# Moving the token factor of a root-mean-square norm behind the matrix product it feeds, in an fp32 two-block transformer kernel

## What is computed

```python
def rms_norm(x, g):
    xf = x.astype(jnp.float32)
    xf = xf * lax.rsqrt(jnp.mean(xf * xf, axis=-1, keepdims=True) + EPS)
    return (xf * g.astype(jnp.float32)).astype(x.dtype)

x = x + rms_norm(mixed, norm1_post[i])
h2 = rms_norm(x, norm2_pre[i])
gate, up = jnp.split(h2 @ w_gate_up[i], 2, axis=-1)     # 1024 -> 2 x 2816
ffn = (jax.nn.silu(gate) * up) @ w_down[i]
x = x + rms_norm(ffn, norm2_post[i])
```

## Time and profile before

| What | Value |
|---|---|
| median of three executions | 2425.7 us (2420.35 to 2428.77) |
| profiled execution, its own time | 2425.2 us |
| span of its trace | 2423.4 us |
| TensorE busy | 2244.8 us, 93% of the span |
| VectorE, ScalarE, GpSimd busy | 46%, 41%, 40% |
| mean granted TensorE clock | 0.949 |
| share of the chain that ended last | TensorE 85%, VectorE 6%, ScalarE 4%, GpSimd 2% |

### The profile page before, as it was taken

One profiled execution on the slowest core, in us unless ns is written; L12 is line 12 of the kernel. 1 busy time (PEld: TensorE's weight loads), 2 busy tenths in 40 slices (PEclk: granted clock), 3 DMA queues, 4 the chain that ended last, 5 costly groups with the idle time before them and its releaser, 6 DMA issues.

```text
span 2423.4 us, 28048 instructions
## 1 busy us (share of the span) xinstructions
PE 2244.8 (93%) x10837; PEld 1837.0 (76%) x10848; DVE 1104.6 (46%) x1784; ACT 984.6 (41%) x1994; POOL 971.7 (40%) x754
## 2 busy tenths in 40 slices
PE   7999999999979887999999798996899997999997
PEld 6788778888867776788888675664687886888886
DVE  3544665553345764755443443445645224332322
ACT  5655444443245553344442354343344233332221
POOL 3654644333466642644334451003423335322232
PEclk9999999999989998999999898887999997999998
DMA  4111122222213220232322111000012221322221
GB/s 161 48 66 53 65 93 94 99 102 96 98 61 96 64 77 18 70 104 87 105 98 96 59 64 35 35 18 18 18 45 82 101 105 37 113 94 105 85 99 60
DMA packets 29845, 183.08 MB, mean 76 GB/s; under 512 B 3984, under 2 KB 4112, under 8 KB 11920
## 3 DMA queue, kind: packets, MB, share of 16 engines
q1 hardware_dynamic: 29712, 181.27, 21.6%
HBM read 174.97 MB, written 2.10 MB: 73 GB/s over the span
## 4 chain that ended last, share of the span: by engine, by line
PE 85%; DVE 6%; ACT 4%; issue 2%; POOL 2%; DMA 1%; SPq 0%; another core or an unknown queue 0%; POOLq 0%; ACTq 0%; DVEq 0%
PE PS L1284 83%; PE PS L1409 1%; PE PS L1519 1%; POOL LO L2486 1%; DVE bQS L1980 1%; POOL A_p L2506 0%; DMA RAW<-wall 0%; DVE aQS L1980 0%; DVE cCVT L2370 0%; POOL A_c L2506 0%; DVE XL L2058 0%; PE PS L1457 0%; POOL bTQ L2539 0%; ACT bP L1820 0%; POOL bROT L2534 0%
## 5 line engine op out<-in xcount | busy, mean ns | idle before, releaser
L2486 POOL TENSOR_TENSOR LO<-RAW,HI 128x512 fp32r<-128x512 f32 (+2 forms) x382 | 538.2, 1425 | 718.9 <-ACT HI L1607 718.9
L1284 PE MATMUL PS<-XH,HI 128*128 128x512 f32 (+1 forms) x1584 | 644.4, 407 | 29.7 <-ACT FP L1903 7.0
L1284 PE MATMUL PS<-XH,LO 128*128 128x512 f32 (+1 forms) x1584 | 627.5, 396 | 0.0
L1284 PE MATMUL PS<-XL,HI 128*128 128x512 f32 (+1 forms) x1584 | 621.7, 397 | 2.2 <-DVE XL L2058 2.2
L1980 DVE TENSOR_TENSOR LO<-RAW,HI 128x512 fp32r<-128x512 f32 (+2 forms) x286 | 303.2, 1064 | 292.1 <-ACT HI L1607 291.9
L1607 ACT ACTIVATE HI<-RAW 128x512 fp32r<-128x512 f32 (+3 forms) x668 | 365.7, 609 | 173.9 <-PE PS L1284 170.4
L1284 PEld LDWEIGHTS PS<-XH,HI 128*128 128x128 f32 (+1 forms) x1584 | 303.6, 192 | 113.4 <-issue 37.8
L1284 PEld LDWEIGHTS PS<-XH,LO 128*128 128x128 f32 (+1 forms) x1584 | 303.2, 191 | 66.5 <-issue 0.8
L1284 PEld LDWEIGHTS PS<-XL,HI 128*128 128x128 f32 (+1 forms) x1584 | 303.4, 192 | 61.6 <-DVE XL L2058 3.7
L1284 PE MATMUL PS<-HH,HI 128*128 128x512 f32 x528 | 205.4, 389 | 0.0
L1284 PE MATMUL PS<-HL,HI 128*128 128x512 f32 x528 | 205.4, 389 | 0.0
(11 more groups left out here) (383 smaller groups left out, 3342.9 us busy)
## 6 DMA issues: line engine op xcount, KB each, us to landing
RAW<-wall SPq DMA_DIRECT2D x138, 1024.0 KB, 4.8
RAW<-wall SPq DMA_DIRECT2D x24, 896.0 KB, 4.4
bROT<-bTQ SPq DMA_DIRECT2D x64, 64.0 KB, 2.0
RAW<-wall SPq DMA_DIRECT2D x5, 512.0 KB, 3.4
XF<-xT SPq DMA_DIRECT2D x4, 512.0 KB, 5.1
outT<-XR SPq DMA_DIRECT2D x8, 256.0 KB, 2.0
FP<-cfp SPq DMA_DIRECT2D x1, 1024.0 KB, 7.1
MKF<-cmask SPq DMA_DIRECT2D x1, 704.0 KB, 10.8
```

Of the source, the lines that this page charges most:

```text
L1284: return e.matmul(out, a, b, start=start, stop=stop)
L2486: return e.tensor_tensor(out, x, h.bitcast(F32), ALU.subtract)
```

## The change

The gain n2pre stays on the operand side, the token factor does not. The new step pv makes XH and XL of block j straight from XR times the gain; ScalarE does XH, VectorE XL (it was GpSimd). pv of block j - 2 stands behind n1 of block j in the list. The add to XR in n1 is on VectorE for blocks 0 and 4 and on GpSimd for the six others. The statistics of "p" become a chore that runs inside the second unit of the up projection: a square with each of the first eight ticks, then two empty ticks, stat0, stats, stat2, an empty tick, stat3, and at the 16th tick a copy of bank 6 to SBUF (RPS, step rps). The sums of squares, of six blocks, are on VectorE (they were on GpSimd). ue2 of units 0 and 1 comes only behind unit 1; each ue2 now begins with two multiplications on VectorE, gate bank by RPS and up bank by RPS, both into SBUF, and Silu runs in place on the first.

```diff
-        for j in range(8):
-            s = put("n1", j)
-            freed[6] = ("n1", s)
-            accumulate("p", j, False)
-        rms_apply("p")
+        for j in range(10):
+            if j < 8:
+                freed[6] = ("n1t", put("n1", j))
+            if j >= 2:
+                x_step[j - 2] = put("pv", j - 2)
         ffn_up("2")
...
+def adder(j):
+
+    return "n1d" if j in (0, 4) else "n1p"
...
     def ffn_up(lay):
+        waiting, scaled = [], [lay != "2"]
+
+        def deviation():
+
+            for j in range(8):
+                accumulate("p", j, False)
+                yield
+            yield
+            yield
+            at_bank(put("stat0", "p", False), 6)
+            yield
+            put("stats", "p", False)
+            yield
+            put("stat2", "p", False)
+            yield
+            yield
+            put("stat3", "p", False)
+            yield
+            freed[6] = ("rps", put("rps"))
+            scaled[0] = True
+
         for j in range(FF):
-            t0, t1 = lin_fm(("up" + lay, j), "X", together=(j == 0))
-            s = put("ue2" if lay == "2" else "ue", lay, j, t0, t1)
...
+            if lay == "2" and j == 1:
+                chores.append(deviation())
+            waiting.append((j,) + tuple(lin_fm(("up" + lay, j), "X", together=(j == 0))))
+            while scaled[0] and waiting:
+                j0, t0, t1 = waiting.pop(0)
+                s = put("ue2" if lay == "2" else "ue", lay, j0, t0, t1)
...
 def scalar(e):
+            elif kind == "pv":
+                j, = a
+                e.wait_ge(*when(adder(j), "n1", j))
+                act(blk(XH, j), blk(XR, j), ACT.Copy, scale=col("n2pre", j)).then_inc(SEM["xh"], 1)
+            elif kind == "rps":
+                e.wait_ge(*when("spr", "stat3", "p", False))
+                act(RPS[:, :], PS[6][:, :], ACT.Copy).then_inc(SEM["rps"], 1)
...
-                act(g, PS[ag.tiles[t0].bank][:, :], ACT.Silu).then_inc(SEM["us"], 1)
+                e.wait_ge(*when("ug", *step))
+                act(g, g, ACT.Silu).then_inc(SEM["us"], 1)
...
 def vector(e):
+            elif kind == "acc" and a[0] == "p" and 0 < a[1] < 7:
...
+                e.tensor_tensor(nb["A2"][:, :], nb["A2"][:, :], nb["SQ" if j % 2 else "MS"][:, :], ALU.add).then_inc(SEM["ac"], 1)
+            elif kind == "pv":
+                j, = a
+                e.wait_ge(*when(adder(j), "n1", j))
+                e.wait_ge(*when("xh", *step))
+                e.scalar_tensor_tensor(out=blk(XL, j), in0=blk(XR, j), scalar=col("n2pre", j), in1=blk(XH, j).bitcast(F32),
+                                       op0=ALU.mult, op1=ALU.subtract).then_inc(SEM["xl"], 1)
...
+                for x, t, name in ((g, t0, "ug"), (v, t1, "uv")):
+                    e.wait_ge(*when_(ag.tiles[t].full))
+                    e.tensor_tensor(x, PS[ag.tiles[t].bank][:, :], RPS[:, :], ALU.mult).then_inc(SEM[name], 1)
                 e.wait_ge(*when("us", *step))
-                e.wait_ge(*when_(ag.tiles[t1].full))
-                e.tensor_tensor(g, g, PS[ag.tiles[t1].bank][:, :], ALU.mult).then_inc(SEM["ud"], 1)
+                e.wait_ge(*when("uv", *step))
+                e.tensor_tensor(g, g, v, ALU.mult).then_inc(SEM["ud"], 1)
...
 def gpsimd(e):
+            elif kind == "n1" and adder(a[0]) == "n1p":
+                j, = a
+                e.wait_ge(*when("n1t", *step))
+                e.tensor_tensor(blk(XR, j), blk(XR, j), blk(YH, j), ALU.add).then_inc(SEM["n1p"], 1)
```

More of the change, by code:

```diff
@@ L173 @@
     "ue": (("ui", 2), ("ud", 2), ("us", 1), ("um", 1), ("hh", 1), ("hl", 1)),
-    "ue2": (("us", 1), ("ud", 1), ("hh", 1), ("hl", 1)),
+    "ue2": (("ug", 1), ("us", 1), ("uv", 1), ("ud", 1), ("hh", 1), ("hl", 1)),
     "lam": (("lamd", 2), ("lama", 1)),
@@ L223 @@
     "cye": (("cye", 1),),
-    "n1": (("n1", 1),),
+    "pv": (("xh", 1), ("xl", 1)),
+    "rps": (("rps", 1),),
 }
@@ L260, in raised @@
         return ((low_part(*step[1:]), 1),)
+    if k == "n1":
+        return ("n1t", 1), (adder(step[1]), 1)
     if k == "ln":
@@ L675, in ffn_up @@
     def ffn_up(lay):
-        for j in range(FF):
-            t0, t1 = lin_fm(("up" + lay, j), "X", together=(j == 0))
-            s = put("ue2" if lay == "2" else "ue", lay, j, t0, t1)
[L679 to L683, removed]
+        waiting, scaled = [], [lay != "2"]
[16 more added lines that the diff above has]
+            scaled[0] = True
+        for j in range(FF):
+            if lay == "2" and j == 1:
[4 more added lines that the diff above has]
+                s = put("ue2" if lay == "2" else "ue", lay, j0, t0, t1)
+                if lay == "2":
+                    freed[tiles[t0].bank], freed[tiles[t1].bank] = ("ug", s), ("uv", s)
+                else:
+                    freed[tiles[t0].bank] = freed[tiles[t1].bank] = ("ud", s)
+                ready["H" + lay, j0] = ("hl", s)
+            assert len(waiting) < 3
     def ffn_down(lay, evac):
@@ L1165, in program @@
     UT["2"] = FP[:, 1152:3200]
+    RPS = sb("RPS", 512, F32, R0 + 104 * K)
     XR = sb("XR", 4096, F32, R0)
@@ L1223, in y_made @@
             return when("la", "ln", "f1", j)
-        return when("n1", "n1", j) if n == "p" else when("cye", *whole["cye", n, j])
+        return when(adder(j), "n1", j) if n == "p" else when("cye", *whole["cye", n, j])
     OPERAND = {"X": (XH, XL), "aO": (aOH, aOL), "bO": (bOH, bOL), "cO": (cOTH, cOTL), "cY": (YTH, YTL), "cM": (MIXH, MIXL)}
@@ L1677, in scalar @@
                 g = UT[lay][:, 1024 * (j % 2):1024 * (j % 2) + 512]
-                if j > 1:
-                    e.wait_ge(*when("hl", *whole["ue2", lay, j - 2]))
-                e.wait_ge(*when_(ag.tiles[t0].full))
-                act(g, PS[ag.tiles[t0].bank][:, :], ACT.Silu).then_inc(SEM["us"], 1)
+                e.wait_ge(*when("ug", *step))
+                act(g, g, ACT.Silu).then_inc(SEM["us"], 1)
                 e.wait_ge(*when("ud", *step))
@@ L2067, in vector @@
                                        op0=ALU.mult, op1=ALU.mult).then_inc(SEM["lt"], 1)
+            elif kind == "acc" and a[0] == "p" and 0 < a[1] < 7:
+                n, j, _ = a
+                nb = NORM[n]
+                e.wait_ge(*when("sq", *step))
+                if j > 1:
+                    e.wait_ge(*when("ac", "acc", n, j - 1, False))
+                e.tensor_tensor(nb["A2"][:, :], nb["A2"][:, :], nb["SQ" if j % 2 else "MS"][:, :], ALU.add).then_inc(SEM["ac"], 1)
[5 more added lines that the diff above has]
+                                       op0=ALU.mult, op1=ALU.subtract).then_inc(SEM["xl"], 1)
             elif kind in ("n1", "fin"):
@@ L2074, in vector @@
                 e.scalar_tensor_tensor(out=y, in0=y, scalar=col("n1post" if kind == "n1" else "n2post", j), in1=PS[6][:, :],
[L2075 to L2080, removed]
+                                       op0=ALU.mult, op1=ALU.mult).then_inc(SEM["find" if kind == "fin" else "n1t"], 1)
+                if kind == "n1" and adder(j) == "n1d":
+                    e.wait_ge(*when("n1t", *step))
+                    e.tensor_tensor(x, x, y, ALU.add).then_inc(SEM["n1d"], 1)
+                elif kind == "fin" and j % 2 == 0:
                     e.wait_ge(*when("find", *step))
@@ L2100, in vector @@
                 lay, j, t0, t1 = a
-                g = UT[lay][:, 1024 * (j % 2):1024 * (j % 2) + 512]
+                u = 1024 * (j % 2)
+                g, v = UT[lay][:, u:u + 512], UT[lay][:, u + 512:u + 1024]
+                if j == 0:
+                    e.wait_ge(*when("rps", "rps"))
+                if j > 1:
+                    e.wait_ge(*when("hl", *whole["ue2", lay, j - 2]))
+                for x, t, name in ((g, t0, "ug"), (v, t1, "uv")):
+                    e.wait_ge(*when_(ag.tiles[t].full))
+                    e.tensor_tensor(x, PS[ag.tiles[t].bank][:, :], RPS[:, :], ALU.mult).then_inc(SEM[name], 1)
                 e.wait_ge(*when("us", *step))
-                e.wait_ge(*when_(ag.tiles[t1].full))
-                e.tensor_tensor(g, g, PS[ag.tiles[t1].bank][:, :], ALU.mult).then_inc(SEM["ud"], 1)
+                e.wait_ge(*when("uv", *step))
+                e.tensor_tensor(g, g, v, ALU.mult).then_inc(SEM["ud"], 1)
                 e.wait_ge(*when("hh", *step))
@@ L2495, in gpsimd @@
                 diff(LO[i % 2][:, c], RAW[i % 2][:, c], HI[i % 2][:, c]).then_inc(SEM["lop"], 1)
-            elif kind == "acc":
+            elif kind == "n1" and adder(a[0]) == "n1p":
+                j, = a
+                e.wait_ge(*when("n1t", *step))
+                e.tensor_tensor(blk(XR, j), blk(XR, j), blk(YH, j), ALU.add).then_inc(SEM["n1p"], 1)
+            elif kind == "acc" and a[0] != "p":
                 n, j, mean = a
```

## The result

| What | Before | Changed |
|---|---|---|
| first timing, median | 2424.2 us (6 runs) | 2415.8 us (6 runs) |
| first timing, ratio | | 0.9966 (0.9953 to 0.9979) |
| second timing, another chip, median | 2424.6 us (22 runs) | 2413.6 us (12 runs) |
| second timing, ratio | | 0.9951 (0.9929 to 0.9973) |
| profiled execution, its own time | 2425.2 us | 2418.2 us |

The change makes the kernel 8 to 11 us faster, where 14.1 had been forecast.

The account below looks back on a forecast made before the run. TensorE bounds the kernel, with a 21.6 us stretch holding none of its large work. Terms: - 17.4 (earlier second unit) + 3.0 (small matmuls) + 0.3 (stat0) = - 14.1 us, so 2411.5 us, range 2405 to 2418.5.

Parts of the forecast that it names:

- Step 1: First unit of the up projection: TensorE needs only XH of block 0 and restarts about 2025.6, 19.3 us earlier.
- Steps 2 to 4: First unit: feed takes 15.6 us, low clock costs nothing beyond it, second unit starts at 2039.9, saving 17.4 us.
- Rival A: First unit: TensorE stays at half clock throughout, second unit 6.3 us later than forecast, 2417.8 us; chance 7%.
- Step 5: Statistics' small matmuls inside TensorE's busy stream add 3.0 us to the path (2.7 to 3.5).
- Step 6: Second unit: last sum of squares at about 2047.2, TensorE at stat0 at 2047.4; 0.3 us allowed (0 to 4.4).
- rival B: Second unit: TensorE waits 4.4 us at stat0 for the sums, 2415.6 us; a clock fall adds 1.4; chance 13%.
- Step 7: ue2's two extra VectorE multiplications: 4.9 us a unit, LO 0.7 later against 6.2 slack, no bank wait, no cost.
- Rivals C and D: C: weights late in every unit, 2431.6 us, 3%. D: nothing starts early, TensorE waits for bank or RPS, 2425, 2%.

Follow-up runs that it names:

- e1: Six empty ticks instead of two before stat0, against the changed kernel: 2410.8 us first, later medians 2404.6 and 2410.3 us.
- e11: Eight empty ticks instead of two before stat0, against the changed kernel: 2408.6 us, 385.70 us behind the mark.
- e7: Four useless 512-column matmuls ahead of stat0 to fill TensorE's wait, against the changed kernel: 2414.7 us.
- e10: stat0 kept in place, stats four ticks behind it instead of one, against the changed kernel: 2410.3 us.
- e5: Squares and sums of "p" moved into the first unit, statistics' matmuls left in place, against the changed kernel: 2416.2 us, ratio 0.9967.
- e6: The six sums of squares back on GpSimd instead of VectorE, against the changed kernel: 2421.4 us.
- e8: On top of e1, the add to XR of block 7 also on VectorE (three there, five on GpSimd): 2410.8 us.
- e9: On top of e1, all eight adds to XR on VectorE, none on GpSimd: 2418.3 us.

## Why the forecast was right in kind and too large in size

Step 1, the restart: forecast mark + 2.4, measured + 2.41.

Steps 2 to 4, the feed and the second unit's start: forecast 15.6 us to the last XL, measured 15.6 (2042.03 + 0.75 - 2027.17); second unit forecast at 17.4 us saved, measured 17.50. The terms inside held in the mean only: an XL was put at 1.05 us; the eight took 0.74 to 1.38, 1.04 in the mean, the ones of 0.74 while GpSimd was idle or just starting. The clock rose at + 7.6 us, 5.2 us behind the restart, between the 2.8 and 6.4 of the two rows used, and cost nothing, as forecast. Rival A did not occur.

Step 5, the small matmuls: forecast 3.0 us, measured 3.0 (e1), with no other effect in the path.

Step 6 is **the step that failed**. "I get the last sum at about 2047.2" was mark + 24.0; it came at + 25.2. TensorE's arrival was forecast to 0.1 us. The term mis-sized is ScalarE's waits for the sums. The step says that squares 3 to 7 wait for the sum two before, but its 6.6 us are eight squares and four HI with no wait between them. In the trace ScalarE waits 1.9 us for sums (0.19 and 1.67), because VectorE's first sum takes 1.11 us and a split of 1.78 stands behind it, ahead of the second. That the split was laid out at 1.4 is only 0.4 of it, an estimate from the two numbers. The wait was 0.95 us and cost 1.1, instead of 0.3. And what a wait there can bring was priced only in rival B, at 13%: "if the clock falls in that gap, 7 matmuls at 0.43 add 1.4 more". It was eight matmuls and 1.6 us, and the fall came 2.8 us behind the wait and not in it. So what came is the forecast's wait, somewhat longer, with B's clock.

Not in the sum at all was the end of the kernel: stat3 at half clock, 0.9 us.

Together: 0.8 + 1.6 + 0.9 = 3.3 us, less 0.1 gained on the start: the difference between the forecast's 14.1 and the 10.95 of the marks. The further 2.6 us between 10.95 and the first median's 8.35 are scatter of the stretches ahead of the mark: the second timing gave 10.95.

Step 7, ue2: RPS came at 2060.4, 33 us behind the mark where about 30 was expected; no bank was waited for. VectorE went to 86.49 us in 196, 4.80 a unit (forecast 4.9). The steady LO ends 5.5 us ahead of the unit that needs it, the forecast's 6.2 less 0.7. VectorE's timeline in a steady unit, which answers to the earlier trace rows; the next unit begins at 2201.7:

```profile
2191.05 0.69 DVE L2161 TENSOR_TENSOR FP<-PS,RPS 128x512 f32<-128x512 f32 x1 [4.68 <-PE PS L1319]
...
2194.80 1.44 DVE L2020 TENSOR_TENSOR LO<-RAW,HI 128x512 fp32r<-128x512 f32 x1 [0.27 <-ACT HI L1642]
```

Rivals C and D are excluded by this and by the restart.

## What to carry to other kernels

A factor that belongs to the columns of a product can be multiplied in behind the product, so that the reduction which gives it no longer stands in front: here that took 17.5 us of waiting away for 3.0 us of small matmuls. Place the reduction where its operands are certain to be ready, and a little later than a layout by hand says. In the changed kernel it stood about a microsecond too early, which cost 2.7 us (1.1 by the wait, 1.6 by the clock); four more ticks, or six (e11), cost nothing. And compare such a change from a mark in the trace just ahead of it, when the scatter of the run is as large as the gain.

## What the runs showed of the hardware that had not been expected

- The clock fell in e7 though TensorE had stopped for no more than 0.2 us: in the 3 us before it had done 18 small matmuls with 3 large ones between. In e10 a stop of 0.95 us did not lower it. The Trainium skill, TensorE: Matmul & The Clock Gate, section on the clock gate, ties the half rate to idleness. e5 and e6 agree with that (falls with waits of 2.5 and 4.9 us), e7 does not by its stop alone; whether the small matmuls are the reason is open, since in e11 they did not lower the clock.
- From the mark on the clock's rises and falls repeat to about 0.2 us for the same program (changed kernel: + 7.62, + 28.10, + 31.52 in one trace, + 7.58, + 28.05, + 31.47 in the other), while in the first 80 us they differ from execution to execution (e1: first fall at 30.6, 32.8 and 36.9 us in its three traces).
- Two-input work of VectorE and of GpSimd slow each other down: 0.744 against up to 1.38 us for an XL, 0.69 against 1.78 for a weight split, and 1.27 against 1.73 for an add on GpSimd. Which of the two pays differs: in e8 and e9 two splits on VectorE took 1.28 us, and GpSimd's two beside them 3.66 and 3.72 where such a pair takes 3.06 in a steady unit. The two engines together were still 0.9 us sooner than VectorE alone.
